# Hybrid RG-LRU and sparse-attention layer: the first norm's scale moved from the activations to the weights, 256-token key pieces, a re-laid memory map, and the latent's variance moved into the first query tile

## The reference

```python
def _rmsnorm(x, g):
    y = x32 * lax.rsqrt(jnp.mean(x32 * x32, axis=-1, keepdims=True) + EPS)
    return (y * g.astype(jnp.float32)).astype(x.dtype)
h = _rmsnorm(x, norm_g[l])
proj = jnp.einsum('bsd,de->bse', h, w_in[l])        # 2048 -> 5456 columns
xa, ga, q, ckv, gb, qi, ki, wi = jnp.split(proj, IN_SPLITS, axis=-1)
# group A: conv of xa, gates, linear recurrence, times silu(ga)
# group B:
c  = _rmsnorm(ckv, ckv_norm_g)                       # 256-wide latent
ki = _layernorm(ki, ik_g, ik_b)                      # 64-wide indexer key
score = jnp.einsum('bqhs,bqh->bqs', jax.nn.relu(jnp.einsum('bqhd,bsd->bqhs', qi, ki)), wi)
_, sel = lax.top_k(score, 256)                       # then attention over the selected latents
```

## Time and profile before

| | |
|---|---|
| median of three runs | 1631.76 us |
| profiled execution, device time | 1631.82 us |
| its span, first to last instruction | 1630.1 us |
| TensorE busy | 1588.7 us, 97% |
| VectorE, ScalarE, GpSimd busy | 854.2, 580.1, 431.7 us |
| mean granted TensorE clock, of full speed | 0.995 |
| TensorE's waits for low weight parts, all tiles | 3.2 us |

### The profile page before, as it was taken

The page is one execution under the profiler, slowest core; times in us unless marked ns, Lnnn a source line. Parts: engine busy times, 40 slices in busy tenths (PEclk is TensorE's granted clock), DMA queues, the critical chain, the costliest instruction groups (busy, mean ns, idle before and its releaser), DMA issues.

```text
span 1630.1 us, 21564 instructions
## 1 busy us (share of the span) xinstructions
PE 1588.7 (97%) x7595; PEld 1324.9 (81%) x7595; DVE 854.2 (52%) x1498; ACT 580.1 (36%) x845; POOL 431.7 (26%) x289
## 2 busy tenths in 40 slices
PE   7999999999999999999999999999998899999998
PEld 7788999888888888888888888777776788888886
DVE  6427555577777877875555555376777100031003
ACT  6325555433444443332111111355555222232321
POOL 2222222222222222222222222110010344444650
PEclk9999999999999999999999999999999999999999
DMA  7212111122212122223222221321222522237322
GB/s 262 83 49 72 46 45 39 33 55 62 61 55 65 33 63 68 68 84 97 77 71 77 71 77 51 110 85 61 71 73 81 217 94 100 94 101 298 132 85 103
DMA packets 132312, 141.38 MB, mean 87 GB/s; under 512 B 8519, under 2 KB 103849, under 8 KB 129961
## 3 DMA queue, kind: packets, MB, share of 16 engines
q1 hardware_dynamic: 130728, 136.55, 26.2%
q0 software_dynamic: 1536, 4.20, 0.8%
HBM read 116.08 MB, written 24.64 MB: 86 GB/s over the span
## 4 chain that ended last, share of the span: by engine, by line
PE 83%; issue 8%; DVE 4%; ACT 2%; POOL 1%; DMA 1%; DVEq 0%; SPq 0%; ACTq 0%; POOLq 0%
PE ps L1039 17%; PE ps L1040 17%; PE ps L1041 17%; PE ps L1315 6%; PE ps L1317 6%; PE ps L1316 6%; PE ps L1142 2%; PE ps L1144 2%; PE ps L1256 2%; PE ps L1220 2%; PE ps L1233 1%; PE ps L1342 1%; PE ps L1341 1%; PE ps L1340 1%; PE ps L1240 1%
## 5 line engine op out<-in xcount | busy, mean ns | idle before, releaser
L1039 PE MATMUL ps<-hT_hi,w_lo 128*128 128x512 f32 (+1 forms) x1344 | 511.9, 381 | 3.2 <-POOL w_lo L663 3.2
L1040 PE MATMUL ps<-hT_lo,w_hi 128*128 128x512 f32 (+1 forms) x1344 | 509.9, 379 | 0.0
L1041 PE MATMUL ps<-hT_hi,w_hi 128*128 128x512 f32 (+1 forms) x1344 | 509.8, 379 | 0.0
L663 POOL TENSOR_TENSOR w_lo<-w_raw,w_hi 128x512 fp32r<-128x512 f32 x168 | 240.7, 1436 | 758.4 <-ACT w_hi L743 758.4
L1039 PEld LDWEIGHTS ps<-hT_hi,w_lo 128*128 128x128 f32 x1344 | 252.6, 188 | 48.6 <-issue 5.4
L1040 PEld LDWEIGHTS ps<-hT_lo,w_hi 128*128 128x128 f32 x1344 | 252.7, 188 | 43.4 <-issue 0.2
L1041 PEld LDWEIGHTS ps<-hT_hi,w_hi 128*128 128x128 f32 x1344 | 252.7, 188 | 42.7
L743 ACT ACTIVATE w_hi<-w_raw 128x512 fp32r<-128x512 f32 x168 | 104.8, 629 | 479.0 <-PE ps L1041 472.7
L1315 PE MATMUL ps<-wo_hi,hT_lo 128*128 128x512 f32 x448 | 175.2, 391 | 3.1 <-DVE hT_lo L1584 3.1
L1643 DVE TENSOR_TENSOR res<-ps,res 128x512 f32<-128x512 f32 x32 | 21.8, 691 | 295.7 <-PE ps L1317 245.0
L1316 PE MATMUL ps<-wo_lo,hT_hi 128*128 128x512 f32 x448 | 174.8, 390 | 0.0
(11 more groups left out here) (190 smaller groups left out, 1825.8 us busy)
## 6 DMA issues: line engine op xcount, KB each, us to landing
w_raw<-in_w_in SPq DMA_DIRECT2D x168, 256.0 KB, 2.8
wo_raw<-in_w_out SPq DMA_DIRECT2D x64, 512.0 KB, 3.6
xin<-in_x SPq DMA_DIRECT2D x8, 1024.0 KB, 6.0
res<-in_x SPq DMA_DIRECT2D x8, 1024.0 KB, 10.6
out<-res SPq DMA_DIRECT2D x16, 512.0 KB, 5.0
y_lru_dram<-sg SPq DMA_DIRECT2D x8, 512.0 KB, 2.8
q_dram<-av SPq DMA_DIRECT2D x8, 512.0 KB, 3.8
gate_dram<-rg SPq DMA_DIRECT2D x8, 512.0 KB, 4.3
```

The lines of the kernel that those rows point to most:

```text
L663: nc.gpsimd.tensor_tensor(w_lo[:, j, :, :], w_raw[:, j, :, :], w_hi[:, j, :, :].bitcast(F32), ALU.subtract).then_inc(w_lo_s, 1)
L1039: nc.tensor.matmul(o, wlo, hi, start=(kt == 0), stop=False)
L1040: nc.tensor.matmul(o, whi, lo, start=False, stop=False)
L1041: return nc.tensor.matmul(o, whi, hi, start=False, stop=(kt == KT - 1))
```

## The change

The gain leaves `norm_x`, whose multiply becomes a `tensor_scalar` with the reciprocal alone; the 1 MB load of `g_bc` becomes an 8 KB load, one transpose on TensorE and a copy to `g_col`, one value for each feature. GpSimd multiplies every piece of raw weights by it, in place, with a broadcast second operand, before ScalarE rounds it; `high` now waits for that multiply (`w_g_s`) in place of the load. x has four buffers, not three. The keys of the first 512 tokens are made in two pieces of 256. The first part of tile 1 takes its high parts one step earlier. The latent's variance goes into tile 3, after its sixth feature block; the root follows on ScalarE, with `high(4, [0])` ahead of it and the other three pieces of tile 4 behind `ki_hi`. Three quarters of the latent's norm go ahead of the first score units. Exp and the decay chain go behind tile 4's score units. The warm-up has 36 transposes. In SBUF small tensors are put ahead of `hT_hi`, `kw_hi` and `kw_lo` get rows of 96, and some tensors change places; every large tensor starts some hundred bytes further on.

```diff
-XB = 3
-FIRST_HALF = NT // P
-WARM = 48
+XB = 4
+WARM = 36
-        kw_hi = s0("kw_hi", [P, KT, KW], F32R)
-        kw_lo = s0("kw_lo", [P, KT, KW], F32R)
+        kw_hi = s0("kw_hi", [P, KT, 96], F32R)[:, :, 0:KW]
+        kw_lo = s0("kw_lo", [P, KT, 96], F32R)[:, :, 0:KW]
@@ SyncE
+            sp.dma_start(g_rows[:, :], a["norm_g"][0].rearrange("(k p) -> k p", p=P)).then_inc(g_in, 16)
             x_load(0)
-            sp.dma_start(g_bc[:, :], a["norm_g"].broadcast_to([P, D])).then_inc(g_in, 16)
...
             x_next(XB)
             x_next(XB + 1)
+            weights(T_C, COL_CKV)
             x_next(XB + 2)
-            weights(T_C, COL_CKV)
             x_next(XB + 3)
-            x_next(XB + 4)
@@ GpSimd
+            def scale_kw(j):
+                pool.wait_ge(w_in_s[j], 16)
+                part = w_raw[:, j, :, 0:KW]
+                nc.gpsimd.tensor_tensor(part, part, gain(j, KW), ALU.mult).then_inc(kw_g_s, 1)
+            pool.wait_ge(g_made, 1)
+            scale_kw(0)
             for j in range(PIECES):
+                if j + 1 < PIECES:
+                    scale_kw(j + 1)
                 cut_kw(j)
             def low(t):
                 for j in range(PIECES):
+                    part = w_raw[:, j, :, :]
+                    pool.wait_ge(w_in_s[j], 16 * t + 16)
+                    nc.gpsimd.tensor_tensor(part, part, gain(j, P), ALU.mult).then_inc(w_g_s, 1)
                     pool.wait_ge(w_hi_s, 4 * t + j + 1)
@@ ScalarE
-                    act.wait_ge(w_in_s[j], 16 * t + 16)
+                    act.wait_ge(w_g_s, 4 * t + j - 3)
-                if FIRST_HALF <= i:
-                    high(1, [i - FIRST_HALF])
+                if 3 <= i < 3 + PIECES:
+                    high(1, [i - 3])
...
+            high(4, [0])
+            act.wait_ge(c_var, 1)
+            nc.scalar.activation(c_rs[:, :], X[1][:, :], ACT.Sqrt, bias=eps[:, :]).then_inc(c_sd, 1)
             act.wait_ge(k_nrm, 1)
...
-            high(4)
-            act.wait_ge(sp_in, 1)
-            nc.scalar.activation(sp_t[:, 1, :], sp_t[:, 0, :], ACT.Exp).then_inc(sp_exp, 1)
-            nc.scalar.activation(c_rs[:, :], X[1][:, :], ACT.Sqrt, bias=eps[:, :]).then_inc(c_sd, 1)
+            high(4, range(1, PIECES))
...
             act_b(T_QI + 1, 0)
+            act.wait_ge(sp_in, 1)
+            nc.scalar.activation(sp_t[:, 1, :], sp_t[:, 0, :], ACT.Exp).then_inc(sp_exp, 1)
@@ TensorE
+            pe.wait_ge(g_in, 16)
+            nc.tensor.transpose(X[0][:, 0:KT], g_rows[:, :], ident[0:KT, 0:KT]).then_inc(g_tp, 1)
...
-                if i < FIRST_HALF:
+                if i in (1, 3):
                     pe.wait_ge(h_lo, 2 * i + 2)
-                    keys_tokens(i * P, P)
+                    keys_tokens((i - 1) * P, 2 * P)
...
+            def latent_variance(kt):
+                if kt != PK + 1:
+                    return
...
+            project_tile(T_QI, 1, 1, between=latent_variance, parts=IX_TOKENS)
@@ VectorE
-                stt(xin[:, i % XB, :], xin[:, i % XB, :], inverse, g_bc[:, :], ALU.mult, ALU.mult
-                    ).then_inc(x_norm, 1)
+                nc.vector.tensor_scalar(xin[:, i % XB, :], xin[:, i % XB, :], inverse, None, ALU.mult
+                                        ).then_inc(x_norm, 1)
...
+            norm_latent(0)
             dve.wait_ge(k_ln, 3)
...
+            norm_latent(1)
+            norm_latent(2)
...
-                    if first and m % 2 == 1 and m < 8:
-                        norm_latent(m // 2)
+                    if first and m == 1:
+                        norm_latent(3)
+            dve_b(T_QI + 1, 0, first=True)
             dve.wait_ge(sp_exp, 1)
...
```

More of the change, by code:

```diff
@@ L145, in layer @@
         causal = sb("causal", [P, P])
[L146 removed]
+        pw = ExitStack()
+        sW = alloc(pw)
+        w_nat = sW("w_nat", [P, QB, IH])
+        par_t = sW("par_t", [P, PARS + 4])
         conv_w = par_t[:, 0:CONV * G].rearrange("p (j g) -> p j g", g=G)
@@ L150, in layer @@
         k_gb = par_t[0:ID, PARS - 2:PARS]
[L151 to L158, removed]
+        decay = sW("decay", [P, 2, G])
+        sp_t = sW("sp_t", [P, 5, G])
+        pw.close()
+        wk_hi = sb("wk_hi", [P, CT, HD], F32R)
         ph = ExitStack()
@@ L1114, in _ @@
             last.then_inc(w_tp, 1)
[L1115 to L1122 removed]
+            def latent_variance(kt):
+                if kt != PK + 1:
+                    return
+                pe.wait_ge(c_sq_s, 2)
+                pe.wait_ge(k_sd, 1)
+                for n in range(2):
+                    for t in range(CT):
+                        last = nc.tensor.matmul(X[1][:, n * NT:(n + 1) * NT], ones_c[:, :],
+                                                c_sq[:, t, n * NT:(n + 1) * NT], start=(t == 0), stop=(t == CT - 1))
+                last.then_inc(c_var, 1)
+            project_tile(T_QI, 1, 1, between=latent_variance, parts=IX_TOKENS)
             def score(t, par, turn, ms, first=False):
@@ L1417, in _, with norm_latent @@
                                     IH ** -0.5 * ID ** -0.5, None, ALU.mult).then_inc(w_nat_s, 1)
+            def norm_latent(j):
+                tok = slice(j * S // 4, (j + 1) * S // 4)
+                if j == 0:
+                    dve.wait_ge(c_sd, 1)
+                chain(nc.vector.reciprocal(c_rs[:, tok], c_rs[:, tok]))
+                for t in range(CT):
+                    stt(c_sb[:, t, tok], c_sb[:, t, tok], c_g[:, t:t + 1], c_rs[:, tok], ALU.mult, ALU.mult
+                        ).then_inc(c_done, 1)
+            norm_latent(0)
             dve.wait_ge(k_ln, 3)
@@ L1420, in _, with stacks, add_scores, dve_b @@
             tt(ki_lo[ID:P, :], k_t[:, :], ki_hi[0:ID, :].bitcast(F32), ALU.subtract).then_inc(ki_done, 1)
+            norm_latent(1)
+            norm_latent(2)
+            def stacks(t, par):
+                dve.wait_ge(st_hi, t * 2 - 2 * (T_QI - 1))
+                a, b = slice(0, ID), slice(ID, P)
+                tt(scored(stack_a[par], b), projected(par, a), scored(stack_a[par], a).bitcast(F32), ALU.subtract)
+                tt(scored(stack_b[par], a), projected(par, b), scored(stack_b[par], b).bitcast(F32), ALU.subtract
+                   ).then_inc(pj_free[par], 1)
+            def add_scores(t, first=False):
+                for m in range(UNITS):
+                    if first and m == 1:
+                        norm_latent(3)
+                    q = FIRST_SCORED + m % (UNITS // 2)
+                    w = (q + 1) * P
+                    k = t * UNITS + (m - UNITS * T_QI)
+                    dve.wait_ge(ix_relu, k + 3)
+                    dve.wait_ge(ix_acc, k + 3)
+                    acc = scores[:, off(q):off(q) + w]
+                    head = t * 2 + (m // (UNITS // 2) - 2 * T_QI)
+                    stt(acc, relu[m % 2][:, 0:w], w_nat[:, q, ds(head, 1)], acc, ALU.mult, ALU.add
+                        ).then_inc(ix_acc, 1)
+            def dve_b(t, par, first=False):
+                stacks(t - 1, 1 - par)
+                add_scores(t - 1, first)
+            dve_b(T_QI + 1, 0, first=True)
             dve.wait_ge(sp_exp, 1)
```

76 lines of the change are left out of this document (26 added, 50 removed).

## The result

The changed kernel takes 1635.12 us (median, 1633.16 to 1637.06), the kernel before beside it 1631.97: a ratio of 1.0017, 95% interval 1.0010 to 1.0023. So it is 3.2 us longer where 4.9 us less was forecast, and outside the forecast range. The profiled execution took 1635.11 us, its span is 1633.4 against 1630.1.

What follows compares the result with a forecast made beforehand. TensorE, working 1588.7 of 1630.1 us, bounds the kernel, so only its waits or slowing can move the time. The start's −6.6 and tile 3's +1.7 sum to −4.9, so 1626.9 us; range 1622.3 to 1632.5.

Steps and rivals of the forecast that it cites:

- The start: Loads to key pieces: keys' second half begins at 56.0 us, not 62.64, so minus 6.6; bounds minus 1.4 and minus 9.5.
- the slow stretch: At the start: TensorE at half clock into the first key piece, adding 0.9 us for some eight products.
- a gain of 1.9 us of products: At the start: two 256-token key pieces cost 12.2 us against 14.1 for four old ones.
- GpSimd's multiply: Four added per tile, 1.3 us each, 1.9 where VectorE works; in the long stages covered by waiting, costing nothing.
- Rival 2: Broadcast multiply costs 3 us and more; gain gone from 3.2, some 1660 us at 4.5; chance 0.13.
- plus 1.0: Around tile 3: tile 4's first scores at 138.0, not 137.02, in times of before, as high(4)'s pieces delay stacks.
- plus 2.6: Tile 5: Exp and decay chain, 4.7 us in series against 2.1 before, make TensorE wait before its first scores.
- Rival 1: Idle gaps at the start cost the clock; start gives only 1.4 to 3.7 us, total 1632.1 to 1629.8; chance 0.20.
- a new wait of 2 to 3 us at tile 5: Sign of being right: TensorE stalls 2 to 3 us before tile 5's first scores.
- where 1.9 was said: Tile 4's scores: one norm piece in front, not four, so the 25.06 us pattern holds: minus 1.9.
- The places: Operands' new places in SBUF: no product's pitch depends on its place, so nothing.
- Rival 3: New operand places shorten products' pitch in the long stages, 10 ns on 5000 products, 50 us: 1577; chance 0.03.

Runs made afterwards that it cites:

- e6: Changed kernel with the order around tile 3 put back as before, keeping the start, the multiplies and the memory map: 1633.42 us, ratio 1.0011 to the kernel before.
- e2: Changed kernel with Exp and decay chain put back before tile 3's end, and norm pieces 1 and 2 back between score units: 1625.71 us, 0.9958.
- e4: Changed kernel without GpSimd's multiplies by the gain, which is left out of the computation: 1628.63 us, ratio 0.9981 to the kernel before.
- e5: Kernel before with only Exp and the decay chain moved late, to where the changed kernel has them: 1637.63 us, ratio 1.0040 to the kernel before.
- e3: Changed kernel with 28 useless identity transposes ahead of tile 4's first score and 48 ahead of tile 5's: 1630.94 us, ratio 0.9992 to the kernel before.
- e10: Changed kernel with small tensors behind causal again and kw_hi, kw_lo rows 80 wide: 1664.89 us, ratio 1.0194 to the kernel before.
- e11: Kernel before with only sums and line_pad (128 bytes) allocated ahead of hT_hi: 1660.38 us, ratio 1.0172 to the kernel before.
- e1: Changed kernel with only Exp and the decay chain put back before tile 3's end: 1627.88 us, ratio 0.9973 to the kernel before.

## Why the prediction was wrong, and where it was right

**The start: right, with other parts.** Said −6.6, measured −7.3. The norm's step is 1.29 us (said 1.3), block 2 landed at 14.01 (14.0), transposes 1 began at 14.22 (13.9). A 256-token key piece took 5.6 us, not 6.1, and the products' pitch was 0.114 us, not 0.127, which I had interpolated as a straight line between 128 and 512 columns. That the slow stretch would hold until the first key piece was right for the changed kernel's profile, and partly luck: the same start had no slow stretch in e6. But I counted the wide pieces as a gain of 1.9 us of products and only noted the idle time that they open; against narrow pieces the whole is a loss of 2.0 to 2.4, of which the profiles put 1.1 on the gaps and the rest on the clock. That step was not worked out for the alternative that stood in the kernel before.

**GpSimd's multiply: size right, cover only half right.** It takes 1.04 us alone and 1.19 on average (said 1.3), and the long stages are untouched: 222 products in 450 to 500 us, and the step of 25.06. Rival 2's price, over 3 us, is refuted. Yet the multiplies cost 6.5 us, in the one place where GpSimd, ScalarE and VectorE work in turns for `stacks`. Rival 2 had the place ("2 us at tile 4's `stacks`" for each microsecond) but hung it on a multiply dearer than it is.

**The first cuts: "plus 1.0" was +2.7** (132.41 against 137.02 less the start's 7.3). The turns of 3.4 us a piece were right (4.4 and 3.2 measured). Missing were the two norm pieces that the change puts ahead of VectorE's `stacks`: the prediction counted them only as a gain for the tile behind, and e2 prices them at 1.7. By e4 what makes them costly is once more GpSimd's work beside them: 2.55 us longer with the multiplies, and next to no cost without. One small sum was also wrong: 60 products of 181 ns are 10.9 us, not 10.6. Nothing rests on it.

**The chain: "plus 2.6" is the term that failed.** The mechanism and the place were named, but the wait is 5.56 us, of which the chain itself is 5.3. I had taken its length from the one row where no GpSimd operation ran beside it, 3.2 us, though the earlier trace rows showed how the two engines stretch each other (3.12 for 1.29) and I had put that contention only on large operations. It acts on eight-element ones as well, which wait 0.6 to 1.1 us. The rest of the term was sound: e4 and e5 wait 4.13 us with 1.0 us of such contention in the chain, and the 3.1 that are left lie 2.7 above before's 0.42, where 2.6 was said. The Trainium skill, "Trainium Architecture — The Big Picture", section "What this means for kernel authors", calls the pair of ports that VectorE and GpSimd share an exclusive lock and not a split of bandwidth; the rows agree, since the addition does not go with the size of the operation that is held up, and the three held operations end with GpSimd's (162.16 against 162.13, for one).

**The clock: no term at all.** Rival 1 named the mechanism, with 0.20, but placed it at the start alone, where the trace of before had shown it. I had forecast a new wait of 2 to 3 us at tile 5 and did not ask what it does to the clock. e3 prices it at 4.2 us. Together: 2.5 too little at the second wait (5.56 less 0.42, against 2.6), 1.7 at the first cuts, 4.2 of clock, and 0.2 for the norm pieces (an estimate: with the waits filled tile 4's step is 30.42, which is 26.95 plus 5.14 less 1.7, where 1.9 was said), less 0.7 more at the start. That is 7.9 of the 8.2 us by which the forecast missed.

**The places: "nothing" was the right sum for a wrong reason.** Both kernels have a distance of 256 or 0 bytes, so nothing changed. But it was not true that the place of an operand doesn't matter, and the change needed its re-laying: with its tensors `w` begins 128 bytes later than before, and with `hT` left at its old place that costs some 30 us (e10; the rows of `kw` can be no more than the last 1.5 us of it, since e11 leaves them alone and costs 28.3). Rival 3 looked at the same thing from the wrong side: the pitch of before was already the fast one.

## What to carry to other kernels

Price a new wait of TensorE as the wait plus the products behind it at the lower clock; here 8.8 us of waiting in two pieces brought 4.2 us more, and filling them with useless transposes gave that back. Before work is moved on VectorE, ask what GpSimd does in the new place, for small operations too: a chain of fourteen operations, most of them 0.17 us long, became 2.1 us longer by three meetings. And when a tensor is added or moved, look at the distance of the two operands of the hot product: 128 bytes off modulo 256 was the largest effect in this study, and no row of waits shows it, only the count of products in a window.

## What the runs showed of the hardware

- Two operands of an fp32r product whose starts are 128 bytes apart modulo 256: 395 ns by the record and 216 products in 50 us, against 389 ns and 222. Two kernels each way (1664.89 and 1660.38 against 1635.08 and 1631.97).
- A 128x8 operation of VectorE beside a two-input operation of GpSimd: 0.72, 0.96, 1.24 and, in e4 and e5, 1.19 us for 0.17. A reciprocal of that size in the same place kept its 0.20.
- GpSimd's multiply with a broadcast operand over 512 elements, in place: 1.04 us, less than its subtraction of the same size (1.26).
- Waits of 3.21 and 5.56 us between dense work lowered the granted clock to 0.64 and 0.57 in the 5 us windows behind them, and one of 3.21 in e1 to 0.89; one of 1.51 us did not (1.00).
